# In the stage of both second-layer attentions VectorE makes a step's pair products ahead of the copy of the step before

## The chip, the cores and the metric

The kernel runs on one core of one Trainium2 chip. The metric is the device time in microseconds (us) of one execution; lower is better. TensorE's clock has two levels here, 1.2 and 2.4 GHz, and the profile gives the granted one as a share of 2.4 GHz (0.50 is 1.2 GHz).

## The reference, cut to what matters

A first block (a recurrent and an attention branch, then an expert layer) comes first; then a second block of two layers. The change lies in the first layer of that second block. For 256 tokens it computes two attentions side by side from one projection:

```python
# gated linear attention, 4 heads of 128 keys and 256 values; b = running sum of log gates
attn[i, j] = sum_k q[i, k] * k[j, k] * exp(b[i, k] - b[j, k])     # for j <= i
o = attn @ v                                                      # then the next sub-block's state
# forgetting attention, 8 heads of 128, in 2 blocks of 128 queries
logits[t, s] = q[t] . k[s] / sqrt(128) + c[t] - c[s]              # c = running sum of log forget gates
o_fox = softmax(where(s <= t, logits, -inf)) @ v
```

## The kernel before, in words

The function `gla_and_fox` is one stage of the program: each engine has its own list of instructions, written out by hand, and semaphores order them among engines. At the end of a stage all engines meet before the next stage starts. The stage runs once. It has 16 steps, j = 0 to 15, and each step does a share of both attentions.

The share of the gated attention: the 256 tokens are cut into 16 sub-blocks of 16. Step j handles, inside every sub-block, the pairs of key j with queries j to 15. VectorE subtracts the log sums (`difference(j)`, line 1896), ScalarE takes the exponential (`pair_exponential`, line 1841), VectorE multiplies by the queries and then by the keys (`products(j)`, lines 1901 and 1902, (16 - j) x 64 columns each), and TensorE adds the products up over the 128 key channels with four matmul records (line 2008). `pair` has three buffers, taken in turn. Beside it ScalarE and GpSimd prepare keys for the blocks between sub-blocks (`kd`, lines 1863 and 1884), and TensorE multiplies them with the queries (lines 2018 and 2021).

The share of the forgetting attention: unit n = j is one head and one half of the queries, 128 keys wide for even n and 256 for odd n. TensorE makes the scores (`score`, lines 1978 and 1979), VectorE scales, masks and takes the maximum (`maxima`, lines 1911 to 1913), ScalarE takes the exponential and the sum (line 1845), VectorE divides (`normalise`, lines 1918 and 1919), TensorE transposes (`turn`, line 1986), ScalarE copies the result out (line 1851), TensorE multiplies by the values (`value`, line 1993), and VectorE copies that out of PSUM (`keep`, line 1924).

TensorE's order in step j is: score(j+1); wait for the pair products of step j (`pdone`), pair matmuls; turn(j), which waits for normalise(j) and for keep(j-1) (`out_done`); the matmuls on `kd`, which wait for GpSimd (`kdone`); value(j), which waits for ScalarE's copy. VectorE's order is: keep(j-1), which waits for value(j-1) (`fx_values`); products(j), which waits for its exponential (`pexp`); normalise(j); maxima(j+1), which waits for score(j+1); difference(j+2), which waits until the matmuls of step j-1 have read their buffer (`pused`). ScalarE's order is: exponential(j), pair exponential (j+1), four exponentials for `kd`, then the copy after turn(j). Nothing in the steps issues a DMA.

After the steps VectorE adds the parts together, TensorE multiplies them by the values, and the next stage (`ab_heads_out`) follows; only the stage behind that one, `ab_out`, asks for its weights by DMA.

Of the kernel before, what the change touches and what calls it, by code (L numbers as in the profile page):

```python
# [1787 lines left out]
def gla_and_fox(st, nc, t, banks, qk, v, la, o, fr, of, con):  # L1788
# [6 lines left out]
    with ExitStack() as own, st.stage() as (block, sem):  # L1795
# [91 lines left out]
        def _(dve):  # L1887
# [4 lines left out]
            def difference(j):  # L1892
                if j >= 3:
                    dve.wait_ge(pused, j - 2)
                n = SUB - j
                nc.vector.tensor_tensor(pair[:, j % 3, :, j:SUB], b3[:, :, j:SUB], b3[:, :, j:j + 1].broadcast_to([P, G * NB, n]), ALU.subtract).then_inc(diff, 1)

            def products(j):
                n = SUB - j
                dve.wait_ge(pexp, j + 1)  # L1900
                link(nc.vector.tensor_tensor(pair[:, j % 3, :, j:SUB], pair[:, j % 3, :, j:SUB], q3[:, :, j:SUB], ALU.mult))
                nc.vector.tensor_tensor(pair[:, j % 3, :, j:SUB], pair[:, j % 3, :, j:SUB], k3[:, :, j:j + 1].broadcast_to([P, G * NB, n]), ALU.mult).then_inc(pdone, 1)
# [3 lines left out]
            def maxima(n):  # L1906
                i, w = n % IT, wide(n)
                dve.wait_ge(scores, n + 1)
                if n >= 2:
                    dve.wait_ge(turned, n - 1)  # L1910
                fx_link(nc.vector.scalar_tensor_tensor(out=s[:, n % 2, 0:w], in0=score_of(n), scalar=scale, in1=mask[:, i, 0:w], op0=ALU.mult, op1=ALU.add))
                fx_link(nc.vector.reduce_max(mx[:, n % 2, 0:1], s[:, n % 2, 0:w], axis=AX.X))
                nc.vector.tensor_single_scalar(mx[:, n % 2, 1:2], mx[:, n % 2, 0:1], -1.0, ALU.mult).then_inc(maxed, 1)

            def normalise(n):
                w = wide(n)
                dve.wait_ge(exps, n + 1)
                fx_link(nc.vector.reciprocal(sums[:, n % 2:n % 2 + 1], sums[:, n % 2:n % 2 + 1]))
                nc.vector.tensor_scalar(s[:, n % 2, 0:w], s[:, n % 2, 0:w], sums[:, n % 2:n % 2 + 1], None, ALU.mult).then_inc(normed, 1)

            def keep(n):
                h, i = divmod(n, IT)
                dve.wait_ge(fx_values, n + 1)
                nc.vector.tensor_copy(of[:, i, h, :], value_of(n)).then_inc(out_done, 1)
# [9 lines left out]
            nc.vector.tensor_tensor(pairs[32:40, :, :], pairs[32:40, :, :], minus[32:40, :].unsqueeze(1).broadcast_to([8, 8, T]), ALU.mult).then_inc(rows_done, 1)  # L1934
            maxima(0)
            for j in range(SUB):
                if j >= 1:
                    keep(j - 1)
                products(j)
                normalise(j)  # L1940
                if j + 1 < N:
                    maxima(j + 1)
                if j + 2 < SUB:
                    difference(j + 2)
# [1140 lines left out]
```

## Time and profile before

| | us |
|---|---|
| median of 3 runs | 3903.57 (3899.72 to 3906.07) |
| profiled execution, its own time | 3912.08 |
| span of that execution | 3909.9 |
| TensorE busy | 3217.6 |
| VectorE busy | 2419.0 |
| ScalarE busy | 1186.7 |
| GpSimd busy | 948.8 |

PE is TensorE, PEld its weight loads, DVE VectorE, ACT ScalarE, POOL GpSimd and SP SyncE. A row of the trace gives the start in us from the span's start, the duration, the engine, the line of the kernel, the operation, the tensors with their shapes, how many instructions stand in the row, and in brackets how long the engine sat idle before it and what ended that. A matmul's end is modelled, and matmuls overlap a little. The stage of the two attentions lies between 2995 and 3140 us of the span.

### The profile page before, as it was taken

What the parts mean: (1) busy time and instruction counts of PE and PEld (TensorE: products, weight loads), DVE (VectorE), ACT (ScalarE), POOL (GpSimd) and SP (SyncE); (2) the same over time, 40 slices, a digit from 0 to 9 for tenths busy, and PEclk for the clock granted to TensorE, in tenths of its full rate; (3) what the DMA queues carried; (4) which work ended last, traced back from release to release, by engine and by line L of the source; (5) the groups of instructions that cost most, each with busy time, mean ns of one, the idle gap of its engine ahead of it and who ended that gap; (6) DMA issues with size and microseconds to landing.
All of it is one profiled execution on the core that took longest, in us unless ns stands there. A gap on an engine that the chain in (4) does not pass through costs nothing. (4 is left out here: it accounts for less than half of the span.)

```text
span 3909.9 us, 39460 instructions
## 1 busy us (share of the span) xinstructions
PE 3217.6 (82%) x13962; PEld 2218.6 (57%) x13962; DVE 2419.0 (62%) x3282; ACT 1186.7 (30%) x1895; POOL 948.8 (24%) x791
## 2 busy tenths in 40 slices
PE   5899998749999947777777777778998878986698
PEld 0688776538797823233333333336886667875587
DVE  2656554658876775665566556556554467769565
ACT  1532122335433511111111111104453344544543
POOL 0000010010000076545555555520000227200100
PEclk7899998879999979999999999999998588998699
DMA  9467322009954599999999999994663044620064
GB/s 389 173 211 287 118 96 90 2 15 370 352 187 147 171 389 427 427 427 427 428 427 428 427 428 428 427 403 138 182 194 109 1 143 144 179 79 1 28 193 145
DMA packets 177392, 942.27 MB, mean 241 GB/s; under 512 B 21532, under 2 KB 26820, under 8 KB 99036
## 3 DMA queue, kind: packets, MB, share of 16 engines
q0 software_dynamic: 82944, 604.02, 37.1%
q1 hardware_dynamic: 94340, 336.94, 26.2%
q8 instruction: 52, 0.85, 0.1%
q14 instruction: 56, 0.46, 0.0%
HBM read 938.78 MB, written 2.10 MB: 241 GB/s over the span
## 5 line engine op out<-in xcount | busy, mean ns | idle before, releaser
L1674 PE MATMUL bank<-pe_v_rows,pe_diag 128*128 128x512 f32 x1920 | 909.0, 622 | 311.3 <-DMA pe_v_rows<-in_expert_v,pe_staged_v 195.3
L1562 DVE SCALAR_TENSOR_TENSOR pe_junk<-pe_u_rows,h_rows 128x2048 f32<-128x2048 f32 x256 | 586.8, 2292 | 453.0 <-DMA pe_u_rows<-in_expert_u,pe_staged_u 442.7
L1674 PEld LDWEIGHTS bank<-pe_v_rows,pe_diag 128*128 128x128 f32 x1920 | 363.1, 197 | 856.5 <-issue 545.8
L1507 POOL DMA_INDIRECT pe_u_rows<-in_expert_u,pe_staged_u x256 | 346.9, 1355 | 227.7 <-DVE pe_junk L1562 79.8
L1507 POOL DMA_INDIRECT pe_v_rows<-in_expert_v,pe_staged_v x248 | 318.7, 1285 | 323.9 <-PE bank L1674 267.9
L1623 ACT ACTIVATE pe_diag<-ident,pe_weights 128x128 f32<-128x128 f32 x240 | 91.5, 399 | 735.3 <-PE bank L1674 735.1
L285 PE MATMUL bank<-h_parts,b_top 128*128 128x512 f32 x768 | 273.0, 400 | 9.2 <-DVE b_rest L386 9.1
L386 DVE TENSOR_TENSOR in_rest<-in_ring,in_top 128x1024 fp32r<-128x1024 f32 x112 | 138.2, 1236 | 220.8 <-ACT in_top L355 220.6
L386 DVE TENSOR_TENSOR c_rest<-c_ring,c_top 128x1024 fp32r<-128x1024 f32 x128 | 174.3, 1369 | 103.0 <-ACT c_top L355 102.7
L386 DVE TENSOR_TENSOR ab_rest<-ab_ring,ab_top 128x1024 fp32r<-128x1024 f32 x112 | 136.9, 1225 | 149.0 <-ACT ab_top L355 148.9
L287 PE MATMUL bank<-h_parts,b_rest 128*128 128x256 f32 x768 | 216.2, 282 | 0.0
L386 DVE TENSOR_TENSOR b_rest<-b_ring,b_top 128x1024 fp32r<-128x1024 f32 x128 | 155.5, 1222 | 85.4 <-ACT b_top L355 85.2
L315 PE MATMUL bank<-in_top,h_parts 128*128 128x512 f32 x640 | 203.3, 398 | 5.6 <-DVE in_rest L386 5.0
L355 ACT ACTIVATE in_top<-in_ring 128x1024 fp32r<-128x1024 f32 x112 | 118.4, 1058 | 286.7 <-PE bank L291 139.2
L285 PE MATMUL bank<-h_parts,c_top 128*128 128x512 f32 x512 | 186.3, 407 | 15.1 <-DVE h_parts L120 10.0
L355 ACT ACTIVATE b_top<-b_ring 128x1024 fp32r<-128x1024 f32 x128 | 135.2, 1058 | 168.6 <-PE bank L287 80.5
L355 ACT ACTIVATE c_top<-c_ring 128x1024 fp32r<-128x1024 f32 x128 | 134.9, 1056 | 143.8 <-PE bank L287 103.4
L285 PEld LDWEIGHTS bank<-h_parts,b_top 128*128 128x128 f32 x768 | 145.0, 189 | 45.9 <-DVE b_rest L386 9.3
L355 ACT ACTIVATE ab_top<-ab_ring 128x1024 fp32r<-128x1024 f32 x112 | 118.3, 1059 | 166.3 <-PE bank L315 84.7
L291 PE MATMUL bank<-h_parts,in_top 128*128 128x512 f32 x512 | 162.1, 397 | 0.0
L315 PE MATMUL bank<-ab_top,h_parts 128*128 128x512 f32 x512 | 158.0, 389 | 0.0
L285 PE MATMUL bank<-h_parts,ab_top 128*128 128x512 f32 x384 | 137.0, 401 | 11.6 <-DVE h_parts L120 11.6
(546 smaller groups left out, 6394.9 us busy)
## 6 DMA issues: line engine op xcount, KB each, us to landing
b_ring<-in_w_mix SPq DMA_DIRECT2D x128, 512.0 KB, 5.4
in_ring<-in_w_in SPq DMA_DIRECT2D x112, 512.0 KB, 4.3
ab_ring<-in_w_ab SPq DMA_DIRECT2D x112, 512.0 KB, 4.1
mod_ring<-in_w_mod SPq DMA_DIRECT2D x32, 1024.0 KB, 8.1
v_rows<-in_w_mod POOLq DMA_DIRECT2D x32, 1024.0 KB, 5.5
k_cols<-in_w_mod POOLq DMA_DIRECT2D x32, 1024.0 KB, 7.1
c_ring<-in_w_c_in SPq DMA_DIRECT2D x64, 512.0 KB, 4.3
c_ring<-in_w_glu_out SPq DMA_DIRECT2D x64, 512.0 KB, 4.5
```

The costliest lines, as they stand in the source:

```text
L285: nc.tensor.matmul(banks[s][:, :].rearrange("p (a t) -> p a t", a=2), fast(weights[0]), fast(seg["both"](k)), start=(k == 0), stop=(k == K ...
L287: mm = nc.tensor.matmul(banks[s][:, 0:T], fast(weights[1]), fast(seg["both"](k)[:, 0, :]), start=False, stop=(k == KT - 1), skip_group_che ...
L291: mm = nc.tensor.matmul(banks[s][:, half * n:(half + 1) * n], fast(weights), fast(seg["rhs"](b, k)), start=(j == 0 and m == 0), stop=(j == ...
L315: mm = nc.tensor.matmul(bank[:, :], fast(seg["lhs"](a, 2 * g + k, t)), fast(weights), start=(g == 0 and k == 0 and m == 0), stop=(g == 7 a ...
L355: nc.scalar.activation(fast(top[:, h % PARTS, :]), ring[:, h % slots, :], ACT.Copy).then_inc(topped, 1)
L386: nc.vector.tensor_tensor(fast(rest[:, h % PARTS, :]), ring[:, h % slots, :], top[:, h % PARTS, :], ALU.subtract).then_inc(split_done, 1)
L1507: gp.indirect_dma_start(buf[:, slot, :], None, table, bass.IndirectOffsetOnAxis(ap=staged[which][:, tile, e:e + 1], axis=0)).then_inc(sems ...
L1562: nc.vector.scalar_tensor_tensor(out=junk[:, :], in0=ub[:, s, :], scalar=1.0, in1=h2tm[:, tile, :], op0=ALU.mult, op1=ALU.mult, accum_out= ...
L1623: nc.scalar.activation(diag[:, e % 4, :], con["ident"], ACT.Copy, scale=wts[:, tile, e:e + 1]).then_inc(diag_done, 1)
L1674: mm = nc.tensor.matmul(banks[4 * tile + b][:, :], diag[:, e % 4, :], vb[:, s, b * 512:(b + 1) * 512], start=False, stop=False, skip_group ...
```

## The change

In each step VectorE issues the pair products of step j first and the copy of step j-1's forgetting-attention values behind them. Step 0 has no copy and is the same. The last copy, behind the loop, stays where it is. No instruction is added, taken away or altered, and the other engines' lists are the same.

```diff
             for j in range(SUB):
+                products(j)
                 if j >= 1:
                     keep(j - 1)
-                products(j)
                 normalise(j)
                 if j + 1 < N:
                     maxima(j + 1)
```

## Rows read from the trace of the kernel before

**Rows 1.** The profile's page: the span and each engine's busy time.

```profile
span 3909.9 us, 39460 instructions
PE 3217.6 (82%) x13962; PEld 2218.6 (57%) x13962; DVE 2419.0 (62%) x3282; ACT 1186.7 (30%) x1895; POOL 948.8 (24%) x791
```

**Rows 2.** Stretches: length, then busy PE, PEld, DVE, ACT, POOL, granted clock, DMA share, GB/s.

```profile
3008.00:3019.17 11.17, 8.62 (x25) 4.21 (x25) 6.72 (x12) 3.04 (x11) 0.32 (x1) 0.53 0.00 0
3019.17:3053.82 34.65, 26.69 (x105) 16.17 (x104) 22.34 (x46) 13.62 (x45) 6.68 (x5) 0.74 0.00 1
3053.82:3085.80 31.98, 27.96 (x99) 21.28 (x99) 16.48 (x36) 10.11 (x34) 7.40 (x5) 0.50 0.00 1
3085.80:3126.16 40.36, 37.57 (x151) 30.91 (x150) 15.55 (x50) 10.99 (x36) 8.35 (x5) 0.50 0.00 1
```

**Rows 3.** Waits of the whole stage: total us, times, longest.

```profile
DVE ab_of L1924 <- PE bank L1993: 52.2, 16, 4.8
PE bank L2008 <- DVE ga_pair L1902: 14.1, 12, 2.0
```

**Rows 4.** TensorE's waits in steps 1 to 5, then 6 to 15.

```profile
PE bank L2008 <- DVE ga_pair L1902: 7.8, 5, 2.0
...
PE bank L2008 <- DVE ga_pair L1902: 6.3, 7, 1.6
PE bank L1993 <- ACT fx_pt L1851: 0.5, 1, 0.5
```

**Rows 5.** TensorE in time: a score in step 3, step 7, then step 10.

```profile
3033.57 0.48 PE L1979 MATMUL bank<-fx_pair,fx_rows 40*128 40x128 f32 x2
...
3060.44 0.77 PE L1993 MATMUL bank<-ab_v,fx_pt 128*128 128x128 f32 x2
...
3061.57 0.79 PE L1979 MATMUL bank<-fx_pair,fx_rows 40*128 40x128 f32 x2
3064.00 2.29 PE L2008 MATMUL bank<-ga_pair,ga_place 128*128 128x288 f32 x4 [1.63 <-DVE ga_pair L1902]
3066.08 0.63 PE L1986 MATMUL bank<-ident,fx_scores 128*128 128x128 f32 x2
...
3086.55 1.22 PE L1979 MATMUL bank<-fx_pair,fx_rows 40*128 40x256 f32 x2
3087.70 1.65 PE L2008 MATMUL bank<-ga_pair,ga_place 128*128 128x192 f32 x4
```

**Rows 6.** VectorE in time: the end of step 6 and the start of step 7.

```profile
3057.79 0.68 DVE L1896 TENSOR_TENSOR ga_pair<-ab_log_sums 128x512 f32<-128x512 f32 x1
3061.26 0.29 DVE L1924 COPY ab_of<-bank 128x128 f32<-128x128 f32 x1 [2.78 <-PE bank L1993]
3061.46 0.75 DVE L1901 TENSOR_TENSOR ga_pair<-ga_pair,ab_qk 128x576 f32<-128x576 f32 x1
3062.25 1.70 DVE L1902 TENSOR_TENSOR ga_pair<-ga_pair,ab_qk 128x576 f32<-128x576 f32 x1
3063.87 0.15 DVE L1918 RECIPROCAL fx_sums<-fx_sums 128x1 f32<-128x1 f32 x1
3064.05 0.35 DVE L1919 TENSOR_SCALAR fx_scores<-fx_scores,fx_sums 128x256 f32<-128x256 f32 x1
```

**Rows 7.** ScalarE in time: the exponential that products(7) waits for.

```profile
3052.29 0.73 ACT L1841 ACTIVATE ga_pair<-ga_pair 128x576 f32<-128x576 f32 x1
```

**Rows 8.** GpSimd in time: its product in step 7.

```profile
3061.84 1.50 POOL L1884 TENSOR_TENSOR ga_kd<-ga_kd,ab_qk 128x512 f32<-128x512 f32 x1 [6.01 <-ACT ga_kd L1863]
```

**Rows 9.** Stretches by clock: columns as in Rows 2.

```profile
3021.90:3025.00 3.10, 3.10 (x4) 1.22 (x5) 1.85 (x5) 0.00 (x0) 0.13 (x1) 0.50 0.00 0
3025.20:3028.40 3.20, 2.49 (x19) 1.47 (x17) 1.58 (x3) 2.49 (x8) 0.23 (x1) 0.99 0.00 0
3049.20:3126.00 76.80, 70.03 (x267) 55.95 (x265) 33.88 (x90) 23.30 (x76) 16.15 (x10) 0.50 0.00 1
```

**Rows 10.** Pair matmuls alone (line 2008), steps 1 to 5: length, PE, PEld, clock, DMA.

```profile
3019.17:3053.82 34.65, 15.11 (x20) 5.60 (x20) 0.74 0.00 1
```

**Rows 11.** VectorE in time: the copy and second product of step 3.

```profile
3033.45 0.29 DVE L1924 COPY ab_of<-bank 128x128 f32<-128x128 f32 x1 [1.88 <-PE bank L1993]
...
3034.71 1.02 DVE L1902 TENSOR_TENSOR ga_pair<-ga_pair,ab_qk 128x832 f32<-128x832 f32 x1
```

**Rows 12.** What starts behind the stage: ScalarE, and the next weights' DMA.

```profile
3140.57 1.91 ACT L2057 ACTIVATE ao_sq<-ab_og 128x2048 f32<-128x2048 f32 x1 [15.72 <-PEq L52]
...
3161.44 1.35 SPq L252 DMA_DIRECT2D ab_out_ring<-in_w_ab_out  x3
```

## The prediction

> **What bounds the kernel now.** I read the page first: TensorE is busy 3217.6 of 3909.9 us and no other engine over 62% [rows 1]. That is an average over stages, so next I took the changed stage alone. It was cut at the starts of the copies on line 1924, which mark the steps: steps 1 to 5, 6 to 9 and 10 to 15 are the last three stretches of [rows 2]. DMA share there is 0.00, so no transfer is involved. In all three TensorE has the most work: 26.69 of 34.65, 27.96 of 31.98 and 37.57 of 40.36 us, against VectorE's 22.34, 16.48 and 15.55.
>
> The list of waits then says who keeps TensorE from being full: 14.1 us in 12 pieces at line 2008, the pair matmuls, waiting for the second pair product [rows 3]. 7.8 us of this lies in steps 1 to 5, 6.3 us in steps 6 to 15; all else TensorE waits for there is 0.5 us, once [rows 4]. In the same list VectorE waits 52.2 us, 16 times, in front of the copy on line 1924 for TensorE's values [rows 3]. So each engine waits for the other in turn: VectorE idles until the values come, copies them, and only then makes products for which TensorE, one score later, is already standing.
>
> Step 7 shows it in time. VectorE finished the difference at 3058.47 (3057.79 + 0.68) and sat 2.78 us until the copy at 3061.26; the products ran from 3061.46 to 3063.95 [rows 6]. TensorE's score was over at 3062.36 (3061.57 + 0.79), and the pair matmuls began at 3064.00, 1.63 us idle [rows 5].
>
> **The change, part by part.** Nothing is added or removed: 15 copies go behind 15 pairs of products, on VectorE's queue only. They pass no DMA and no other queue.
>
> (a) The products come earlier. Products(7) need their exponential, finished at 3053.02 (3052.29 + 0.73) [rows 7], and VectorE, free from 3058.47. At the length that they had, 2.49 us even with the slow one of 1.70, they end at 3060.96, before the copy can start at all (3061.26) and 1.4 us before the score ends [rows 6]. The wait of 1.63 goes whole. The tightest kind of step is an early one: in step 3 the idle time before the copy was 1.88 us and the products took 2.07 (from 3033.66, right behind the copy, to 3034.71 + 1.02) [rows 11]. There the copy slips by 0.2 us at first, and by up to about 1.6 more as TensorE comes earlier by what the step in front has saved (7.8 / 5 = 1.57). That does not pile up: VectorE's work is 22.34 / 5 = 4.5 us a step, TensorE's without its waits (34.65 - 7.8) / 5 = 5.4 [rows 2, 4], so VectorE catches up. From step 6 on it is (31.98 + 40.36 - 6.3) / 10 = 6.6 against (16.48 + 15.55) / 10 = 3.2 [rows 2, 4].
>
> So all 12 waits go: 14.1 us [rows 3]. The idle time is counted from the modelled end of a score, and where nothing waits the pair matmuls start 1.15 us behind the row of the second score operand, though that row is 1.22 long (3086.55 to 3087.70) [rows 5]: 0.07 more for each wait, 12 x 0.07 = 0.8. Sum 14.9 us. Bounds of this term from the same rows: 0, if each wait is filled by another, and 14.9.
>
> (b) The copy comes later, by at most the products' length. Who waits for it is turn(j), which also needs normalise(j), queued behind it. From the copy's start to the end of the division takes, without the products between, 0.2 (3061.26 to 3061.46) + 0.18 (3063.87 to 3064.05) + 0.35 = 0.73 us [rows 6]. TensorE has the score and the pair matmuls to do before turn: in step 7 that is 3060.44 + 0.77 = 3061.21 to 3062.29 and then 2.08 us (3064.00 to 3066.08), together 3.2 us [rows 5]. So the products may end up to 3.2 - 0.7 = 2.5 us behind the values before anything waits; (a) has them end 0.3 us ahead. Cost taken: 0. It can't be a gain, as the copy is never earlier; its worst case is R5 below.
>
> (c) ScalarE and GpSimd: their orders stay. Their busy time is 13.62 and 6.68 in 34.65 us [rows 2]; with steps of 5.4 us they need 2.7 and 1.3 a step. 0.
>
> (d) The products on line 1902 took 1.70 us where the one on line 1901, of the same shape, took 0.75, and GpSimd's product ran from 3061.84 to 3063.34 over just that time [rows 6, 8]. Such holds now fall on whatever VectorE does when GpSimd starts. In step 7 the moved products are over by 3060.96, so the hold goes to the division or a difference. The division has 2.5 us of room from (b), and the hold is worth 1.70 - 0.75 = 0.95: 0.
> The Trainium skill, SBUF — State Buffer, section Who interferes with whom, says that a VectorE instruction with two SBUF inputs and a GpSimd instruction that reads SBUF exclude one another for the whole instruction, whoever came first. By that rule GpSimd can lock out the division too, which speaks against moving it late; the sum stays as it is as long as the room of (b) holds, which the trace has for the wide steps and which is smallest in the last ones.
>
> (e) TensorE's clock. In steps 1 to 5 it changes level about every half step: 0.50 while the pair matmuls run (3021.9 to 3025.0), 0.99 for the small matmuls behind them (3025.2 to 3028.4); from 3049.2 on it is 0.50 throughout, at 91% busy [rows 9]. Without the gaps the steps are shorter and these changes fall elsewhere. Both ends by rows: if steps 1 to 5 went wholly at 1.2 GHz, their small matmuls, 26.69 - 15.11 = 11.6 us [rows 2, 10], would stretch like the score's 0.79 against 0.48 [rows 5], by 0.65 x 11.6 = 7.5 us. If the pair matmuls went at 2.4 GHz too, 15.11 us [rows 10] would shrink by up to 7.5, but VectorE's 22.3 us then become the bound in place of TensorE's 26.8: 26.8 - 22.3 = 4.5, less an estimated 0.3 us a step for hand-offs, some 3 us gained. I take a quarter of the loss, 1.9 us: the present half-and-half is the nearest row, and a shift can lose more than it wins.
>
> What is saved in the stage reaches the end: the next stage starts at a meeting of all engines, and the next big weights are asked for only at 3161.44, behind it [rows 12].
>
> Sum: 14.9 - 0 - 0 - 0 - 1.9 = 13.0 us. Against the profiled execution's own 3912.08 that is 3899.1. That execution is 8.5 us over the median of the runs, so for the median: 3903.57 - 13.0 = 3890.6 us, 0.33% faster.
>
> **Rivals.** A measurement of this kernel can tell about 0.2%, 7.8 us, from no change.
>
> R1, the clock sticks at 1.2 GHz in steps 1 to 5: 14.9 - 7.5 = 7.4, with some of it spared 6 to 10 us, so about 3895.6. For it: the level was lost for good at 3049.2 with TensorE busy [rows 9]. Against: the widest pair matmuls, behind which it rose, are in just these steps.
>
> R2, the denser TensorE gets 2.4 GHz for more of the time: 14.9 + 3 in steps 1 to 5, and up to 9 more if steps 6 to 9 came to it (27.96 / 1.65 = 17 us of work, VectorE's 16.48 beside it, against 27.96 now [rows 2]): 17 to 27 us, about 3882. For it: steps without idle time. Against: 0.50 for 76.8 us at 91% busy [rows 9].
> The Trainium skill, TensorE: Matmul & The Clock Gate, section What's actually happening, says that the slow clock is the default and activity releases it; by that rule removing idle time can only help, while this trace shows a busy stretch that stayed slow.
>
> R3, the wait comes back in part: in steps 1 to 5 VectorE doesn't catch up (the 1.6 us slip of (a) against a score of 0.8 to 1.2), or holds by GpSimd meet the products and then the division. Half of the 7.8 us and more stays: gain 0 to 6, about 3900. Against: 4.5 us of work in a step of 5.4.
>
> R4, it doesn't do what it says: products(j) still can't start before the values, since their exponential or VectorE comes too late. 3903.6. Against: 3053.02 against 3061.26 [rows 6, 7].
>
> R5, slower: the ready copy is held behind products that wait for their exponential, and turn(j), which needs it, is late. It decides where products end more than 2.5 us behind the values. To be slower by 7.8 us it must also eat the gain: (14.9 + 7.8) / 15 = 1.5 us more in every step, products ending 4 us behind the values, so some 4.3 us later than (a) has them. Time then 3912. ScalarE's exponential would have to come 9 us later than it does [rows 7].
>
> **How the numbers follow.** Forecast (gain 10 to 17) 0.50; R1 0.18; R2 0.12; R3 0.12; R4 0.04; R5 0.04. Faster by over 0.2%: the forecast, R2 and most of R1 (0.15): 0.77. Slower: R5, 0.04. Within: the rest, 0.19. The range goes from a gain of 20.6 to one of 5.6, 3883 to 3898: it holds the forecast, all of R1, over half of R2 and a little of R3, 0.8 together; the forecast's own is 3886.6 to 3893.6.
>
> **What would show it.** Right: the list of waits has under 2 us at line 2008 behind line 1902; the pair matmuls start 1.15 us behind the row of line 1979 for 256 columns; VectorE's idle time stands before the copy still, but between products and copy, some 35 us; step 7 takes 6.4 us from copy to copy. The clock in steps 1 to 5 tells between the forecast (0.6 to 0.8), R1 (0.5) and R2 (over 0.85). R3 shows as a wait at line 2008 or at line 1986 for line 1919. Wrong would be: waits gone and the stage as long, or a new wait of turn.

## The result, and the profile after

| | before | changed | ratio of the runs |
|---|---|---|---|
| median of 5 runs, us | 3906.07 (3899.72 to 3913.27) | 3873.82 (3867.78 to 3888.95) | 0.9921 [0.9908, 0.9935] |
| profiled execution, its own time | 3912.08 | 3888.95 | |

That is 31 us faster (25 to 36 by the interval), where 13 were forecast. Run again beside other kernels on one chip it gave 0.9930 [0.9916, 0.9944], 27 us. The profiled execution of the changed kernel is the slowest of its five, 15 us above their median, so what its trace gives for the steps is rather too long than too short.

First the page of the changed kernel. TensorE is busy 17.6 us less, though it does the same matmuls [rows 1].

```profile
span 3886.8 us, 39460 instructions
...
PE 3200.0 (82%) x13962; PEld 2214.2 (57%) x13962; DVE 2416.3 (62%) x3282; ACT 1188.0 (31%) x1895; POOL 938.8 (24%) x791
```

Then the stage, cut at the copies as in [rows 2], but into steps 1 to 8 and 9 to 15: the kernel before, for which this is a new cut, and the changed one. Columns are the length, then busy PE, PEld, DVE, ACT, POOL, granted clock, DMA.

```profile
3019.17:3077.58 58.41, 47.32 (x174) 31.20 (x172) 35.44 (x72) 21.26 (x69) 11.93 (x9) 0.64 0.00 0
3077.58:3126.16 48.58, 44.90 (x181) 37.16 (x180) 18.93 (x59) 13.46 (x44) 10.50 (x6) 0.50 0.00 1
```

```profile
3025.45:3059.80 34.35, 32.15 (x174) 21.41 (x172) 31.08 (x73) 21.32 (x69) 8.14 (x9) 0.94 0.00 1
3059.80:3104.98 45.18, 44.52 (x181) 37.16 (x180) 17.52 (x56) 13.47 (x44) 11.22 (x6) 0.50 0.00 1
```

From first copy to last the steps take 79.5 us in place of 107.0: 27.5 us less, 24.1 of them in steps 1 to 8. The first column less the second is what TensorE idled: 11.1 before and 2.2 now in steps 1 to 8, 3.7 and 0.7 behind them. So 11.9 us of the 27.5 are waits. Nearly all of the rest is TensorE's busy time in steps 1 to 8, 47.3 against 32.2 us for the same 174 records, at a granted clock of 0.94 in place of 0.64. That is the part I hadn't forecast. The repeat gives a second profile of the changed kernel, with the clock at 1.00 in all of steps 1 to 8 and its steps 1 to 15 in 75.9 us, 31.1 less than before:

```profile
3019.80:3053.87 34.07, 30.49 (x174) 20.39 (x172) 31.83 (x73) 21.58 (x69) 8.18 (x8) 1.00 0.00 1
3053.87:3095.70 41.83, 40.78 (x181) 34.22 (x179) 18.91 (x57) 13.58 (x45) 11.23 (x6) 0.57 0.00 1
```

The waits of the changed kernel (total us, times, longest), against [rows 3, 4]; the 14.1 us are 1.6:

```profile
DVE ab_of L1924 <- PE bank L1993: 24.7, 10, 4.2
...
PE bank L2008 <- DVE ga_pair L1902: 1.6, 2, 1.0
...
PE bank L1993 <- ACT fx_pt L1851: 0.5, 1, 0.5
PE bank L2018 <- POOL ga_kd L1884: 0.4, 1, 0.4
```

And step 2 in time, TensorE and then VectorE. The pair matmuls start 0.65 us behind the row of the score, no wait between, and four of 448 columns take 1.77 us; in the kernel before the narrower ones of step 7 took 2.29 [rows 5].

```profile
3029.64 0.70 PE L1979 MATMUL bank<-fx_pair,fx_rows 40*128 40x256 f32 x2
3030.29 1.77 PE L2008 MATMUL bank<-ga_pair,ga_place 128*128 128x448 f32 x4
3031.90 0.27 PE L1986 MATMUL bank<-ident,fx_scores 128*128 128x128 f32 x1
```

```profile
3029.14 1.09 DVE L1902 TENSOR_TENSOR ga_pair<-ga_pair,ab_qk 128x896 f32<-128x896 f32 x1
3030.15 0.28 DVE L1924 COPY ab_of<-bank 128x128 f32<-128x128 f32 x1
3030.35 0.15 DVE L1918 RECIPROCAL fx_sums<-fx_sums 128x1 f32<-128x1 f32 x1
3030.54 0.29 DVE L1919 TENSOR_SCALAR fx_scores<-fx_scores,fx_sums 128x128 f32<-128x128 f32 x1
```

VectorE has no idle time in front of this copy, nor of five more of the eight in steps 1 to 8. In the first profile the two engines are about equally full there (31.1 and 32.2 of 34.35 us); in the repeat, at 1.00, VectorE is the fuller one, 31.8 against 30.5 of 34.07 us, and so the bound.

### The profile page after: what moved, and what is told of

It is laid out like the page before. It is cut to its first block and busy times, and to the rows that moved or that the text cites. A ratio compares the mean times of both kernels' runs of the same rounds, so it can differ in the third digit from the quotient of the medians.

```text
span 3886.8 us, 39460 instructions
## 1 busy us (share of the span) xinstructions
PE 3200.0 (82%) x13962; PEld 2214.2 (57%) x13962; DVE 2416.3 (62%) x3282; ACT 1188.0 (31%) x1895; POOL 938.8 (24%) x791
## 5 line engine op out<-in xcount | busy, mean ns | idle before, releaser
L285 PE MATMUL bank<-h_parts,c_top 128*128 128x512 f32 x512 | 187.3, 409 | 14.1 <-DVE h_parts L120 9.7
```

The lines of the kernel that those rows point to most:

```text
L285: nc.tensor.matmul(banks[s][:, :].rearrange("p (a t) -> p a t", a=2), fast(weights[0]), fast(seg["both"](k)), start=(k == 0), stop=(k == K ...
```

## The experiments

Theory A: removing the waits let TensorE keep 2.4 GHz in steps 1 to 8, and that is half of the gain. Theory B: only the waits count and the rest came from elsewhere. Each kernel has one profile; its stage times come from that, its ratio from 4 to 12 runs against the kernel before.

**1. Where the gain lies: one part of the steps at a time.** The condition is `j <= 8` in the first and `j > 8` in the second.

```diff
-                products(j)
+                if j <= 8:
+                    products(j)
                 if j >= 1:
                     keep(j - 1)
+                if not (j <= 8):
+                    products(j)
```

> The products stand ahead of the copy in steps 1 to 8 only; steps 9 to 15 as before. Theory A (the missing waits let TensorE keep 2.4 GHz in steps 1 to 8, and that is half of the gain): nearly the whole gain of the change stays, 26 to 29 us (ratio about 0.993), steps 1 to 8 take 34 to 38 us with a granted clock over 0.85, and waits of about 3.2 us at line 2008 are back in steps 9, 11, 13 and 15. Theory B (only the waits count, 14.9 us in all, the rest of the measured gain comes from elsewhere): 14.9 - 3.4 = 11.5 us (0.997).

> The products stand ahead of the copy in steps 9 to 15 only; steps 1 to 8 as before. Theory A: the clock is at 1.2 GHz there either way, so only the waits of steps 9, 11, 13 and 15 go: 3.2 us, with 0.07 each 3.4 us (ratio 0.999). Theory B gives the same here, 3.4 us; a gain over 8 us would say that the late steps hold a part of the gain that neither names.

Early: 3883.79 us, 0.9944 [0.9931, 0.9957], 22 us faster; steps 1 to 15 took 83.7 us, 23.3 less. Late: 3905.38 us, 0.9999 [0.9989, 1.0008]; 103.8 us, 3.2 less. Steps 1 to 8 of the early one are those of the changed kernel again, with its clock:

```profile
3013.63:3048.27 34.64, 32.44 (x174) 21.51 (x172) 29.90 (x70) 21.39 (x69) 8.28 (x9) 0.93 0.00 1
3048.27:3097.32 49.05, 44.90 (x181) 37.16 (x180) 19.42 (x59) 13.47 (x44) 10.99 (x6) 0.50 0.00 1
```

The waits of the late steps are back, four of them with 3.6 us. B's 11.5 us lie outside the interval, which is 17 to 27 us; A's 26 to 29 meet only its upper end. By stage times the two parts add up, 23.3 + 3.2 = 26.5 of 27.5; by the ratios they give 22 of 27 to 31, where each interval is 4 to 5 us wide either way.

**2. The clock without the order.** The kernel before, with two filler matmuls where TensorE idles.

```diff
+                if 1 <= j <= 8:
+                    for _ in range(2):
+                        nc.tensor.matmul(banks[4][:, :].rearrange("p (g t) -> p g t", g=2)[:, :, 0:P], con["ident"], place[:, 0:2, :], start=True, stop=True, skip_group_check=True)
                 pe.wait_ge(pdone, j + 1)
```

> VectorE's order is that of the kernel before; TensorE gets two more matmuls (128x256, fp32, constants, into columns of bank 4 that nothing reads) in front of its wait for the pair products in steps 1 to 8, where it idles now. Theory A: the granted clock in steps 1 to 8 rises from 0.65 to over 0.85, the pair matmuls take half as long (1.9 us in step 1 in place of 3.5), and since VectorE's order keeps its wait, 1 to 1.5 us a step are saved in 5 to 8 steps, less 1 to 3 us where the fillers are longer than the gap: 5 to 10 us faster (0.998). Theory B, with the clock without effect: 0, or slower by the fillers' overhang, up to 5 us.

3896.18 us, 0.9965 [0.9951, 0.9979], 14 us faster by doing more work; steps 1 to 15 took 91.4 us, 15.6 less. Its steps 1 to 8, where TensorE still idles 3.6 us:

```profile
3020.46:3062.54 42.08, 38.44 (x206) 25.87 (x204) 34.78 (x73) 21.28 (x69) 10.75 (x8) 1.00 0.00 1
```

The clock alone, with VectorE's order as before, is worth over half of the change's gain by the stage times (15.6 of 27.5) and about half by the ratios (14 of 27 to 31), more than I expected (5 to 10). B is wrong here too.

**3. The order with the idle time put back.** A wait on TensorE alone, in the changed kernel, of two lengths: for `maxed, j + 2`, and for `diff, j + 3`.

```diff
+                if 1 <= j <= 8:
+                    pe.wait_ge(maxed, j + 2)
                 pe.wait_ge(pdone, j + 1)
```

> The changed kernel with one more wait on TensorE: in steps 1 to 8 the pair matmuls wait for maxima(j+1) on VectorE, 1.1 us behind the score. Theory A: idle time of about 1.1 us is back in each of the eight steps (9 us), and the clock falls back to some 0.6 there (10 to 12 us more), so that little of the gain is left: 3 to 12 us faster than the kernel before (0.997 to 0.999). Theory B: the eight waits cost their own 9 us and no more: 22 us faster than before (0.9945), with the clock no part of it.

> The changed kernel with a longer added wait on TensorE: in steps 1 to 8 the pair matmuls wait for difference(j+2) on VectorE, some 1.7 to 2.1 us behind the score, as long as the waits of the kernel before (1.2 to 2.0 us in its steps 1 to 5). With the wait of 1.1 us the clock had stayed up. Theory A (the length of the gap decides: with gaps as before the clock falls as before): a granted clock of 0.6 to 0.75 in steps 1 to 8 and 0.50 in the last of them; steps 1 to 15 take 100 to 106 us, 1 to 7 us less than before. Theory B (gaps cost their own length only, and the clock fell in the kernel before for another reason): 79.5 us and 8 x 1.9 = 15 make 95, the clock over 0.85.

The short one: 3895.36 us, 0.9966 [0.9953, 0.9979], 13 us faster than before. Its waits, and its steps 1 to 8:

```profile
PE bank L2010 <- DVE fx_max L1913: 8.3, 8, 1.2
```

```profile
3025.36:3067.86 42.50, 33.91 (x174) 23.11 (x172) 33.48 (x72) 21.20 (x69) 10.10 (x9) 0.90 0.00 1
```

The clock stayed at 0.90 and the gaps cost 8.2 us (87.7 against 79.5), their own 8.3: A as I had put it, that such a gap brings the slow clock back, missed; B's stage time fits, though its 22 us for the whole kernel does not (13, 8 to 18). Against the repeat's 75.9 us the gaps cost 11.8, so how much over their own length they cost stays open.

The long one: 3909.37 us, 1.0006 [0.9991, 1.0022]. The whole gain is gone, though the products are early:

```profile
PE bank L2010 <- DVE ga_pair L1896: 13.9, 8, 2.0
```

```profile
3017.93:3076.36 58.43, 44.44 (x174) 29.71 (x172) 33.06 (x72) 21.27 (x69) 9.53 (x9) 0.69 0.00 0
3076.36:3121.55 45.19, 44.53 (x181) 37.16 (x180) 16.93 (x57) 13.47 (x44) 10.51 (x6) 0.50 0.00 1
```

Steps 1 to 8 take 58.43 us, as the kernel before did (58.41), and the clock is 0.69, in steps 7 and 8 at 0.50. Between the two kernels the idle time grew by 5.6 us (8.3 to 13.9) and the steps by 15.9 (42.50 to 58.43); the difference is TensorE's busy time, 33.9 against 44.4. Only the length of the gap differs between the two: in these profiles 1.0 us a step left the clock up and 1.7 us lost it, and the ratios, 0.9966 and 1.0006, are clear of each other.

**4. The clock in the late steps.** In steps 9 to 15 the changed kernel has 0.50 with next to no idle time. Fillers again, as in experiment 2, under `if j >= 7`; and in another kernel the key products between sub-blocks in falling order (ScalarE, GpSimd and TensorE each take `r = NB - m` for the widths and columns in place of m; GpSimd's part is shown), so that wide goes with wide.

```diff
             for m in range(1, NB):
                 gp.wait_ge(kexp, G * m)
-                nc.gpsimd.tensor_tensor(kd[:, m % 3, :, 0:SUB * m], kd[:, m % 3, :, 0:SUB * m], k[:, :, 0:SUB * m], ALU.mult).then_inc(kdone, 1)
+                r = NB - m
+                nc.gpsimd.tensor_tensor(kd[:, m % 3, :, 0:SUB * r], kd[:, m % 3, :, 0:SUB * r], k[:, :, 0:SUB * r], ALU.mult).then_inc(kdone, 1)
```

> The changed kernel with two more matmuls (128x256, fp32, constants, into columns of bank 4 that nothing reads) in front of the pair matmuls of steps 7 to 15. Theory A (what TensorE is given decides its clock; the late steps have too little for it): the clock stays at 1.00 past step 8, each late step takes 5 to 5.5 us in place of 6.5 to 7.5 in spite of 0.9 us of fillers: 8 to 14 us faster than the changed kernel (0.989 of before). Theory B (fillers can't hold it there): the clock is 0.50 and each filler pair costs 1.7 us at 1.2 GHz: 12 to 15 us slower than the changed kernel (0.996).

> The changed kernel with the key products between sub-blocks (kd: ScalarE, GpSimd, TensorE) in falling order: the widest (240 columns) in step 0, the narrowest (16) in step 14, so that wide pair products go with wide kd and narrow with narrow. If TensorE's clock stays at 2.4 GHz in steps 1 to 8, VectorE bounds them (3.7 to 4.7 us a step) and the wide kd matmuls, 1.9 us at that clock, nearly fit beside it, with waits for GpSimd of up to 1 us in each early step; steps 9 to 14 lose most of their kd work, 3 us in the last of them: steps 1 to 15 take 66 to 75 us in place of 79.5, 5 to 13 us faster than the changed kernel (0.989 to 0.991 of before). If the wait for GpSimd is the bound, the early steps take 5.5 us and the gain is eaten: 79 us.

Fillers: 3875.9 us, 0.9921 [0.9903, 0.9939]; steps 1 to 15 took 72.5 us. Falling order: 3870.87 us, 0.9917 [0.9896, 0.9938]; 66.5 us. Steps 9 to 15 of the first (steps 14 and 15 are slow again), then steps 3 to 5 and 6 to 15 of the second:

```profile
3051.78:3089.45 37.67, 36.33 (x209) 30.36 (x207) 23.22 (x56) 14.08 (x46) 11.26 (x6) 0.85 0.00 1
```

```profile
3029.64:3052.86 23.22, 23.09 (x84) 16.66 (x85) 13.34 (x28) 8.39 (x25) 5.04 (x4) 0.56 0.00 0
3052.86:3084.95 32.09, 30.27 (x201) 22.27 (x199) 27.37 (x83) 18.19 (x68) 7.75 (x9) 1.00 0.01 1
```

Both stages are shorter than the changed kernel's 79.5 and 75.9 us, and the fillers again go with a raised clock. But neither ratio is clear of the changed kernel's 0.9921: the further 8 to 14 and 5 to 13 us that I had expected are seen in the steps of one profile each, not in the runs.

The row of 23.22 us shows the other side: TensorE is busy 23.09 us of it, without a gap, and still slow. I tried to hold it with one filler in steps 1 to 5, then with two in steps 2 to 8, beside the falling order and the changed kernel once more each; and the falling order with VectorE's order of before.

> The changed kernel with the kd work in falling order, and one filler matmul (128x256, fp32, constants) in front of the pair matmuls of steps 1 to 5. In falling order alone the clock fell to 0.50 in steps 3 to 5, which took 23.2 us in place of some 14. If one filler holds the clock there, 9 us less, at 0.45 us for each filler: steps 1 to 15 take 58 to 62 us in place of 66.5, and the kernel is 4 to 8 us faster than in falling order (0.990 of before). If not, the fillers cost 2 to 4 us: 69 us.

> Changed order, kd in falling order, two fillers (128x256, fp32) in front of the pair matmuls of steps 2 to 8. With one filler in steps 1 to 5 the clock fell in step 4 and stayed down to step 13. If two hold it where it fell, steps 1 to 15 take 64 to 70 us (0.990 of before); if the clock falls all the same, as in the run with one, 88 to 95 us (0.996).

> Changed order with kd in falling order, unaltered, in another execution. If the clock takes the course that it took (0.50 to 0.65 in steps 3 to 5, else 1.00): 66.5 us for steps 1 to 15 and 0.9917 of before. If the course differs from execution to execution, as it did with the filler: up to 85 us.

> The changed kernel again, unaltered, beside the others on the same chip, for its ratio and for whether the clock takes the same course in another execution. 0.992 of before; steps 1 to 15 take 79 to 88 us, the clock at 1.00 in most of steps 1 to 8.

> VectorE's order of the kernel before, with the kd work in falling order. If TensorE's idle time before the pair matmuls is what costs the clock, it stays near 0.75 in the first steps in spite of the wider kd matmuls, and the gain over before is only what the light late steps save, 10 to 20 us (0.995 to 0.997). If what it is given decides alone, the clock stays over 0.9 as with the changed order, and steps 1 to 15 take under 80 us.

| kernel | median us | ratio | steps 1 to 15, us |
|---|---|---|---|
| falling, one filler, steps 1 to 5 | 3879.3 (3859.58 to 3890.13) | 0.9910 [0.9887, 0.9933] | 85.4 |
| falling, two fillers, steps 2 to 8 | 3870.52 (3868.69 to 3874.23) | 0.9901 [0.9886, 0.9915] | 62.8 |
| falling again | 3869.14 (3863.86 to 3898.32) | 0.9917 [0.9891, 0.9943] | 66.0 |
| changed kernel again | 3880.79 (3874.9 to 3891.62) | 0.9930 [0.9916, 0.9944] | 75.9 |
| falling, order of before | 3914.88 (3907.19 to 3920.48) | 1.0009 [1.0000, 1.0017] | 107.5 |

With one filler the clock fell in step 4 and stayed down to step 13 in the profiled execution, as the second row shows. That was a slow one, though: its six runs go from 3859.58, the fastest of all kernels here, to 3890.13 us, and it had 3887.75. So one filler may well have held the clock in others; the profiles don't show it. With two it was 1.00 over all fifteen steps.

```profile
3020.63:3038.68 18.05, 16.54 (x94) 11.49 (x93) 17.63 (x28) 9.83 (x27) 5.83 (x3) 1.00 0.00 1
3038.68:3105.99 67.31, 66.52 (x262) 49.56 (x260) 36.17 (x102) 23.59 (x86) 11.11 (x11) 0.55 0.00 1
```

```profile
3017.20:3080.03 62.83, 60.11 (x373) 45.46 (x371) 54.22 (x129) 33.42 (x112) 17.16 (x14) 1.00 0.00 1
```

The kernel with falling order and VectorE's old order is a strong sign that the waits and the clock belong together: TensorE waits 15.3 us at the pair matmuls, the clock is 0.55 over all steps, and it is no faster than before; with the new order the same work takes 66 us in place of 107.5. My 10 to 20 us for it were wrong.

The version with two fillers has the lowest ratio, 0.9901, and the narrowest spread, 5.5 us over only 4 runs. Its interval ends just short of that of the repeated changed kernel and overlaps that of its first measurement: that it beats the changed kernel is likely, not shown.

## Why the prediction was wrong

The direction, the waits of (a), which are the smaller part of the gain, and the row that they were read from held; step (e), the clock, failed in size and in sign, and with it the sum: it was put at a loss of 1.9 us and gave back 15.2 us of TensorE's busy time. Of the signs named, the wait at line 2008 came out (1.6 us); step 7 takes 3.65 us from copy to copy where 6.4 were named, and VectorE idles 24.7 us before the copy, not 35.

- **(a), the waits at line 2008.** 14.1 us were to go wholly; 1.6 stayed, in two steps, and with new small waits TensorE's idle time fell by 11.9 us where I had 14.9. The cause is in the condition of (a): VectorE would catch up because TensorE's steps are 5.4 us. In steps 1 to 5 of the first profile they are 4.1 (20.58 / 5, in the row under (e)) beside VectorE's 4.2, and in the repeat, over steps 1 to 8, 3.8 beside 4.0: VectorE had nothing left to catch up with. The copy slips as foreseen: in step 2 it starts right behind the products.
- **(b), the copy late.** 0 was right: in the first profile nothing waits for line 1919 or for the copy, in the second 0.5 us.
- **(c) and (d), ScalarE, GpSimd, holds.** For TensorE right to 0.4 us (one wait for GpSimd). In step 7 the products take 0.75 and 0.76 us now, as the rows below show, where the second took 1.70 [rows 6]. The holds moved as (d) has it: over the stage the products on lines 1901 and 1902 took 28.3 us before and 23.4 now, the divisions on line 1919 6.5 before and 7.5 now, 10.2 in the repeat. (d) put this at nothing because the division has room; with VectorE the bound its time counts as well, and TensorE waits 0.5 us for it in the repeat.

```profile
3049.94 0.75 DVE L1901 TENSOR_TENSOR ga_pair<-ga_pair,ab_qk 128x576 f32<-128x576 f32 x1
3050.73 0.76 DVE L1902 TENSOR_TENSOR ga_pair<-ga_pair,ab_qk 128x576 f32<-128x576 f32 x1
```

In the repeat a division of 128 columns took 0.28 us in step 2, and 0.84 in step 4, where GpSimd's product ran beside it:

```profile
3024.89 0.28 DVE L1919 TENSOR_SCALAR fx_scores<-fx_scores,fx_sums 128x128 f32<-128x128 f32 x1
3033.62 0.84 DVE L1919 TENSOR_SCALAR fx_scores<-fx_scores,fx_sums 128x128 f32<-128x128 f32 x1
```

```profile
3033.53 0.86 POOL L1884 TENSOR_TENSOR ga_kd<-ga_kd,ab_qk 128x320 f32<-128x320 f32 x1 [3.72 <-ACT ga_kd L1863]
```

- **(e), the clock.** Taken: 1.9 us lost, between 7.5 lost and 3 gained. Measured: TensorE's busy time fell by 15.2 us in steps 1 to 8. Two things were wrong. The upper end was cut off at step 5; I let the clock reach steps 6 to 9 only in R2, worth 9 us more, and gave that 0.12. Of the 15.2 us, 6.1 lie in steps 1 to 5 (26.69 to 20.58) and 9.1 in steps 6 to 8. For steps 1 to 5 the upper end was near: they take 22.27 us in place of 34.65, 12.4 less, of which 7.8 are the waits and 4.6 are left for the clock, where I had some 3. And "the nearest row" was no ground for half-and-half: [rows 9] show the granted clock at 0.99 right after the dense pair matmuls and 0.50 after the idle time. Two rows alone didn't prove cause and effect, but the idle time was what the change took away. I read instead the 76.8 us at 0.50 and 91% busy as evidence against. It is evidence that light late steps can stay slow once the clock is down, as in experiments 1 and 4, and says little of the steps with wide pair matmuls.

```profile
3025.45:3047.72 22.27, 20.58 (x107) 12.91 (x106) 20.76 (x45) 13.31 (x44) 4.30 (x5) 0.92 0.00 1
```

- **R2** was the case that came: the upper end of its 17 to 27 us is near the stage's 27.5, though its time of about 3882 is still 8 us over the measured median, and it named the clock of over 0.85 that was to tell it (0.94 measured). R1 and R5 did not occur. My range ended at a gain of 20.6 us, in the middle of R2.

The rule quoted with R2, that activity releases the slow clock (the Trainium skill, TensorE: Matmul & The Clock Gate, section What's actually happening), was the better guide; the runs agree with it both ways (fillers 0.64 to 1.00, long gaps 0.94 to 0.69), and I set it below a row from another kind of step. It isn't the whole of it: 23.09 of 23.22 us busy at 0.56 (experiment 4) is activity with the clock still slow, and why is open.

What stays open: the ratios of the changed kernel (27 and 31 us) and of the kernel with the short gap (13 against 19 us of its stage) leave a few us either way that one profile each can't place. Outside of steps 1 to 15 the fourteen profiled executions take 3796 to 3809 us, the same kernel in two executions 6 to 7 us apart, so such remainders say nothing of the change. The clock's course also differs between executions: the changed kernel lost it for good in step 8 in one profile and in step 10 in the other.

## What to carry to other kernels

Where TensorE waits a little in every step and its granted clock is well below full, price a removed wait twice: once for its length, once for the busy time around it that may run at 2.4 GHz; here the second was larger (15 against 12 us). Then look for the engine that bounds the steps at the fast clock, since it caps the gain. And a few useless matmuls in the idle time are a cheap test of it: if they raise the granted clock and make the kernel faster, the clock is the lever.

## What I had not expected of the hardware

- A gap of 1.0 us in each of eight steps left the clock at 0.90, one of 1.7 us brought it to 0.69: 5.6 us of idle time cost 15.9 us.
- Being busy isn't enough: 23.09 of 23.22 us busy at a clock of 0.56, and 66.5 of 67.3 us at 0.55; in the profile with two matmuls of 128x256 more in each of steps 2 to 8 all these steps ran at 1.00.
- The level outlasts its cause. With falling order the matmuls of steps 9 to 13 are the same with and without fillers in the steps in front, yet with VectorE's new order they ran at 0.50 in the profile where the clock had fallen in step 4 and at 1.00 in the three others; step 9 took 5.55 and 3.18 us in two of them:

```profile
3074.74:3080.29 5.55, 5.55 (x23) 4.85 (x23) 3.54 (x9) 2.45 (x10) 0.99 (x1) 0.50 0.00 0
```

```profile
3064.97:3068.15 3.18, 3.04 (x22) 2.62 (x22) 2.97 (x10) 2.16 (x9) 1.00 (x1) 1.00 0.00 0
```

- The single runs of one kernel lie up to 34 us apart (3863.86 to 3898.32, falling order), and 5.5 us apart in the four runs with two fillers. That the clock's course makes the difference fits the profiles but isn't shown, as each set of runs has only one.
